# One function table in a page loop, an output norm moved up, and the last steps of a recurrence in other slots

## The chip, the cores and the metric

The kernel runs on one core of a Trainium2 chip. The metric is the device time of one launch in microseconds (us), as the median of several runs. Before the change it was 1774.12 us (three runs, 1769.87 to 1775.15).

## The reference, cut to what matters

The kernel computes one inference step of a hybrid decoder layer for a prompt of 512 tokens and for 8 decoding sequences that share the weights. Two parts of it are worked on at the same time in the loop that is changed.

The first is the latent attention of the 8 decoding sequences over their cached pages, 32 pages of 128 rows each. The keys are made from the cached rows, normalised per head, and scored:

```python
def page_step(carry, phys):
    c_blk = ckv_pool[phys]
    kp_blk = kpe_pool[phys]
    s = mla_scores(q_nope, q_pe, mla_keys(c_blk, p), kp_blk)   # mla_keys: rms_norm(c @ W) per head
    return update(carry, s, c_blk), None                       # running softmax
```

The second is the chunked gated-delta recurrence of the prompt (4 heads). Its triangular inverse is built level by level, then per chunk, with `state` carried on:

```python
v_new = u_i - w_i @ s
o = q_i @ s + a_i @ v_new
s = s * exp(gl) + k_i.T @ v_new
y = rms_norm(o, g) * silu(z)
```

Both norms are a reciprocal root, which the kernel computes on ScalarE as exp(-0.5 * ln(mean + eps)). The softmax needs exp as well.

## The kernel before, in words

The pages' loop has four iterations. One iteration takes two sequences, that is 64 pages, and one chunk of the recurrence. The 64 pages are the slots 0 to 63 of the iteration; slots 0 to 31 belong to the first sequence (r = 0), slots 32 to 63 to the second (r = 1). The order of the work on every engine is written out by hand: in each slot an engine does its part of one page and then whatever small steps the tables of slot numbers (`S_K` ... `S_OT`, `S_LVL`, `SLOT_*`) place there. Engines wait for each other by semaphores.

The page itself is a pipeline. In slot n TensorE (PE) first transposes page n + 1 (`turn_page`, L1324 to L1326; L1324 only in odd slots), then multiplies page n by the key weights (`page_products`, two groups of six matmuls, L1343; in odd slots also two small ones, L1341). ScalarE (ACT) copies the transposed page n + 1 out of the bank (`take_high`, L1511), VectorE (DVE) makes the low part of it (`take`, L1673; for even pages also a copy, L1672), and the products of page n + 1 in the next slot wait for that. ACT then squares the products of page n (L1523, L1526), and DVE sums the squares (L1683). What an engine has to do besides for its slot comes after this, and so stands in front of the next page's L1511 or L1673.

The steps that come besides are these. `values` on PE in slots 9 to 17 and 41 to 49 (L1357), `latent` in slots 19 and 51 (L1366). `soften` on ACT: Ln in slots 0 and 32 (L1478), Exp in slots 1 and 33 (L1481), the softmax's four Exps in slots 7 and 39 (L1486); on DVE the four instructions of the maximum in slots 2 and 34 (L1583 to L1588). The recurrence (`gdn`) has its PE matmuls in the slots of the tables: keys and values transposed in slots 3 and 5 (L1376, L1382), levels of the inverse at `S_LVL` (first number L1409 on PE and a copy L1493 on ACT; second number L1415 and L1418 on PE, then DVE steps L1636 in that slot and L1640 in the one after), then W, U, Q, O, S and the transposed output OT (L1453). The DVE steps at the end of a chunk are: the output's second term added (L1643 and L1647), squared (L1650), summed (L1653), the state scaled (L1656) and added to (L1659), the output normalised (L1662) and, after OT, multiplied by the gate (L1665). ACT does Ln (L1502) and Exp (L1505) of the output norm.

ScalarE evaluates a function from a table set that has to be loaded. The kernel asks for the set `exp_and_others` ahead of the loop, by `exp_only` (L265); every Ln in the loop then has an ACT_TABLE_LOAD ahead of it, and so has the Exp behind it. `log_exp` (L261) asks for the set `natural_log_exp_and_others`, which holds both; other blocks of the kernel use it.

After the loop the softmax of the last sequence is done once more by the same lines (L1478, L1481, L1583 and so on), with nothing else to do; then the next block starts.

Of the kernel before, what the change touches and what calls it, by code (L numbers as in the profile page):

```python
# [131 lines left out]
def build_in(nc, io, ctx):  # L132
# [130 lines left out]
    def exp_only(act):  # L263

        nc.scalar.preload_act_table_set("exp_and_others")  # L265
# [968 lines left out]


    S_K, S_V, S_A, S_QK, S_L0 = 3, 5, 6, 7, 10
    S_LVL = [(13, 16), (19, 22), (25, 28), (31, 35), (41, 44), (47, 50)]
    S_W, S_U, S_Q, S_O, S_S, S_OT = 52, 54, 55, 57, 58, 63
    assert len(S_LVL) == LEVELS - 1 and S_OT < 2 * PAGES

    p_w = sem("weights_split")
    with nc.Block() as block:
        @block.sync
        def _(sp):

            sp.wait_ge(p_w, 1)
            sp.dma_start(qpair[0:RO, :, 0, :], qps).then_inc(sem("pair_in"), 16)
            sp.dma_start(qpair[RO:P, :, 1, :], qps).then_inc(sem("pair_in"), 16)
            sp.wait_ge(sem("pair_in"), 32)

        @block.vector
        def _(dve):
            st = Steps(dve, sem("prelude_dve"))
            nc.vector.memset(qpair, 0.0).then_inc(p_w, 1)
            for k in range(2):
                raw = w3[:, k, :, :]
                for n, (dst, lo, hd) in enumerate(((wka4, H, 0), (wkb4, 0, 2))):
                    hi_v = dst[:, 0, k, lo:lo + 2 * HD].rearrange("p (h w) -> p h w", h=2)
                    lo_v = dst[:, 1, k, lo:lo + 2 * HD].rearrange("p (h w) -> p h w", h=2)
                    st(nc.vector.tensor_copy(hi_v, raw[:, hd:hd + 2, 0:HD]))  # L1260
                    st(nc.vector.tensor_tensor(lo_v, raw[:, hd:hd + 2, 0:HD], hi_v.bitcast(F32), ALU.subtract))
                st(nc.vector.tensor_copy(wvv[:, k, :].rearrange("p (h w) -> p h w", h=H), raw[:, :, HD:2 * HD]))
            st(nc.vector.tensor_copy(qsplit5[:, 0, :, :, :].rearrange("p b k h -> p (b k h)"), keep[:, 0:64]))
            st(nc.vector.tensor_tensor(qsplit5[:, 1, :, :, :].rearrange("p b k h -> p (b k h)"), keep[:, 0:64],
                                       qsplit5[:, 0, :, :, :].rearrange("p b k h -> p (b k h)").bitcast(F32), ALU.subtract))
            for v in (bank[0], bank[1], bank[4], bank[5], state):
                nc.vector.memset(v[:], 0.0)
            dve.sem_inc(loop_ready, 1)
            dve.sem_inc(p_e, PAGE_CREDIT)
            dve.sem_inc(p_r, PAGE_CREDIT)  # L1270
            dve.sem_inc(g_st, 1)
            dve.sem_inc(g_y, 1)
            dve.sem_inc(b_lat, 1)

        @block.gpsimd
        def _(pool):
            for v in (cpage[1][:, 0:PAGES // 2, :], ssq[1], nope[1], lat, score):
                nc.gpsimd.memset(v[:], 0.0)

        @block.scalar  # L1280
        def _(act):
            exp_only(act)
            other = cpage[1][:, PAGES // 2:PAGES, :].rearrange("p n c -> p (n c)")
            nc.scalar.activation(other, bc(ones[:, 0:1], P, PAGES // 2 * KL), ACT.Copy, scale=0.0)
            act.sem_inc(p_qa, 1)
            act.sem_inc(p_qb, 1)

        @block.tensor
        def _(pe):
            pe.sem_inc(p_kb, PAGE_CREDIT)  # L1290
            pe.sem_inc(b_pv, 1)
            pe.sem_inc(g_qs, 1)

    with nc.Block() as block:
# [177 lines left out]
        @block.scalar  # L1472
        def _(act):
            def soften(slot, m, q):

                if slot == SLOT_SOFT:
                    act.wait_ge(p_r, m * PAGES + PAGE_CREDIT)
                    nc.scalar.activation(ssq[q][:], ssq[q][:], ACT.Ln, scale=1.0 / HD, bias=eps[:]).then_inc(sem("soft_ln"), 1)  # L1478
                if slot == SLOT_SOFT + 1:
                    act.wait_ge(sem("soft_ln"), m + 1)  # L1480
                    nc.scalar.activation(ssq[q][:], ssq[q][:], ACT.Exp, scale=-0.5).then_inc(b_rs, 1)  # L1481
                if slot == SLOT_EXP:
                    act.wait_ge(b_nb, m + 1)
                    act.wait_ge(b_pv, m + 1)
                    for h in range(H):
                        nc.scalar.activation(prob[:, :, h], score[:, :, h], ACT.Exp, bias=pmax[:, 8 + h:9 + h], scale=MLA_SCALE,  # L1486
                                             accum_out=rsum[:, bass.ds(m, 1), h]).then_inc(b_exp, 1)

            def gdn(slot, c):
                for n, (sm, sd) in enumerate(S_LVL):  # L1490
                    if slot == sm:
                        act.wait_ge(g_m, c * (LEVELS - 1) + (n + 1))
                        nc.scalar.activation(mlev.rearrange("p h w -> p (h w)"), G1[:], ACT.Copy).then_inc(g_mr, 1)  # L1493
                if slot == S_W:
                    act.wait_ge(g_w, c + 1)
                    nc.scalar.activation(wneg.rearrange("p h w -> p (h w)"), G0[:], ACT.Copy, scale=-1.0).then_inc(g_we, 1)
                if slot == S_U:
                    act.wait_ge(g_vn, c + 1)
                    nc.scalar.activation(vnew, G1[:], ACT.Copy).then_inc(g_vne, 1)
                if slot == S_S + 2:  # L1500
                    act.wait_ge(g_ss, c + 1)
                    nc.scalar.activation(osm[:, 0:4], osm[:, 0:4], ACT.Ln, scale=1.0 / HD, bias=eps[0:CH, :]).then_inc(sem("gdn_ln"), 1)  # L1502
                if slot == S_S + 3:
                    act.wait_ge(sem("gdn_ln"), c + 1)
                    nc.scalar.activation(osm[:, 4:8], osm[:, 0:4], ACT.Exp, scale=-0.5).then_inc(g_rs, 1)  # L1505

            def take_high(i, r, n):
                g = i * (2 * PAGES) + (r * PAGES + n)
                act.wait_ge(p_t, g + 1)
                act.wait_ge(p_kb, page_free(g))  # L1510
                nc.scalar.activation(turned[n % 2][:, 0:KL], bank[n % 2][:, 0:KL], ACT.Copy).then_inc(p_hi, 1)  # L1511

            take_high(0, 0, 0)
            with act.Fori(0, NB // 2) as i:
                for r in range(2):
                    b = 2 * i + r
                    for n in range(PAGES):
                        g = i * (2 * PAGES) + (r * PAGES + n)
                        take_high(i, r, n + 1)
                        act.wait_ge(p_ka, g + 1)  # L1520
                        act.wait_ge(p_r, page_free(g))
                        key_at, score_at = (H, 0) if r == 0 else (0, 2 * HD)
                        nc.scalar.activation(square[n % 2][:, 0:2 * HD], bank[2][:, key_at:key_at + 2 * HD], ACT.Square)  # L1523
                        nc.scalar.activation(nope[r][:, n, :], bank[2][:, score_at:score_at + H], ACT.Copy).then_inc(p_qa, 1)
                        act.wait_ge(p_kb, page_done(g))
                        nc.scalar.activation(square[n % 2][:, 2 * HD:4 * HD], bank[3][:, 0:2 * HD], ACT.Square).then_inc(p_qb, 1)  # L1526
                        soften(n, b, 1 - r)
                        gdn(r * PAGES + n, i)
            soften(SLOT_SOFT, NB, 1)
            soften(SLOT_SOFT + 1, NB, 1)  # L1530
            soften(SLOT_EXP, NB, 1)
# [44 lines left out]
        def _(dve):  # L1576
# [32 lines left out]
            def gdn(slot, c):  # L1609
# [34 lines left out]
                if slot == S_O:  # L1644
                    dve.wait_ge(g_av, c + 1)
                    dve.wait_ge(g_o1, c + 1)
                    nc.vector.tensor_tensor(o1, G1[:], o1, ALU.add).then_inc(chain, 1)  # L1647
                if slot == S_S:
                    dve.wait_ge(chain, c * 3 + 1)
                    nc.vector.tensor_tensor(osq, o1, o1, ALU.mult).then_inc(chain, 1)  # L1650
                if slot == S_S + 1:
                    dve.wait_ge(chain, c * 3 + 2)
                    nc.vector.tensor_reduce(osm[:, 0:4], heads(osq), AX, ALU.add).then_inc(g_ss, 1)  # L1653
                if slot == S_S + 2:
                    dve.wait_ge(g_kv, c + 1)
                    nc.vector.tensor_tensor(heads(state), heads(state), col(elast[:, bass.ds(c * H, H)], P, H, HD), ALU.mult).then_inc(chain, 1)  # L1656
                if slot == S_S + 3:
                    dve.wait_ge(chain, c * 3 + 3)
                    nc.vector.tensor_tensor(state, G0[:], state, ALU.add).then_inc(g_st, 1)  # L1659
                if slot == S_OT - 1:  # L1660
# [862 lines left out]
```

## Time and profile before

| | us |
|---|---|
| median of three runs | 1774.12 (1769.87 to 1775.15) |
| profiled execution, its own time | 1768.66 |
| span in the profile | 1766.9 |
| PE busy | 1571.0 (89%) |
| DVE busy | 812.6 (46%) |
| ACT busy | 656.7 (37%) |

The profiled execution is 5.5 us shorter than the median of the runs. The busy shares are means over the whole kernel; the changed loop runs from about 395 to 1056 us after the span's start, and in it PE has hardly any gap. PEld is TensorE's weight load, which comes ahead of each matmul; where a row of it has an idle time in brackets, PE had nothing to go on with.

### The profile page before, as it was taken

The numbers are of one execution on the slowest core, as the hardware profiler recorded it, in microseconds if no ns is written. First come the engines' busy times: TensorE is split into PE (matmuls) and PEld (weight loads), VectorE is DVE, ScalarE is ACT, GpSimd is POOL, SyncE is SP. The second block draws the span as 40 slices with busy tenths as digits, with TensorE's granted clock in tenths as the row PEclk, the third lists the DMA queues.
The fourth block names the chain that finished last, engine by engine and source line by source line (L and its number), as shares of the span: only waits on it lengthen the run. The fifth ranks groups of instructions, "written<-read, shape, count | busy, mean of one in ns | idle before, by whom it ended". The sixth has DMA issues, their size and how long they took to land. (4 is left out here: it accounts for less than half of the span.)

```text
span 1766.9 us, 31133 instructions
## 1 busy us (share of the span) xinstructions
PE 1571.0 (89%) x10945; PEld 1300.4 (74%) x10945; DVE 812.6 (46%) x1552; ACT 656.7 (37%) x1660; POOL 65.0 (4%) x77
## 2 busy tenths in 40 slices
PE   2999667619998999899989997999888999998999
PEld 2599434318988898888989883534443999998998
DVE  2311577765555554655565551332566222224321
ACT  3022234445545555545454560000123333334121
POOL 0000000030000000000000000000000000000000
PEclk8999886869999999999999997899889999999999
DMA  7022000022313131313222207124203233331331
GB/s 235 0 75 69 15 0 1 23 63 54 91 42 89 39 93 45 89 38 87 53 70 57 65 1 257 59 63 187 107 1 97 72 95 95 95 86 50 89 102 55
DMA packets 190622, 128.29 MB, mean 73 GB/s; under 512 B 49240, under 2 KB 175953, under 8 KB 190468
## 3 DMA queue, kind: packets, MB, share of 16 engines
q1 hardware_dynamic: 190476, 126.52, 24.8%
q8 instruction: 70, 1.15, 0.3%
q14 instruction: 76, 0.62, 0.1%
HBM read 120.20 MB, written 6.37 MB: 72 GB/s over the span
## 5 line engine op out<-in xcount | busy, mean ns | idle before, releaser
L1343 PE MATMUL bank<-wka,turned 128*128 128x260 f32 x1536 | 252.4, 300 | 15.9 <-DVE turned L1673 13.8
L1683 DVE TENSOR_REDUCE arena<-arena 128x4 f32<-128x512 f32 x256 | 175.6, 686 | 183.9 <-ACT arena L1526 183.3
L1343 PE MATMUL bank<-wkb,turned 128*128 128x256 f32 x1536 | 237.6, 291 | 0.0
L1343 PEld LDWEIGHTS bank<-wka,turned 128*128 128x128 f32 x1536 | 203.2, 192 | 27.1 <-DVE turned L1673 24.5
L1343 PEld LDWEIGHTS bank<-wkb,turned 128*128 128x128 f32 x1536 | 202.7, 192 | 0.0
L2276 PE MATMUL bank<-h_high,ffn_high 128*128 128x260 f32 x704 | 142.5, 284 | 3.0 <-DVE h_low L2334 3.0
L2276 PE MATMUL bank<-h_low,ffn_high 128*128 128x260 f32 x704 | 142.7, 284 | 0.0
L2276 PE MATMUL bank<-h_high,ffn_low 128*128 128x260 f32 x704 | 142.1, 284 | 0.0
L1511 ACT ACTIVATE turned<-bank 128x256 fp32r<-128x256 f32 x257 | 98.3, 382 | 109.2 <-PE bank L1326 109.2
L1673 DVE TENSOR_TENSOR turned<-bank,turned 128x256 fp32r<-128x256 f32 x257 | 107.1, 417 | 56.1 <-ACT turned L1511 56.1
L1526 ACT ACTIVATE arena<-bank 128x256 f32<-128x256 f32 x256 | 98.7, 386 | 89.4 <-PE bank L1343 89.4
L1523 ACT ACTIVATE arena<-bank 128x256 f32<-128x256 f32 x256 | 98.3, 384 | 80.1 <-PE bank L1343 78.5
L1750 PE MATMUL bank<-arena,yT 128*128 128x512 f32 (+1 forms) x240 | 121.7, 644 | 4.3 <-DMA arena<-in_w_mix_out 3.9
L2276 PEld LDWEIGHTS bank<-h_high,ffn_high 128*128 128x128 f32 x704 | 109.4, 190 | 3.1 <-issue 3.1
L2276 PEld LDWEIGHTS bank<-h_low,ffn_high 128*128 128x128 f32 x704 | 109.1, 190 | 0.0
L2276 PEld LDWEIGHTS bank<-h_high,ffn_low 128*128 128x128 f32 x704 | 109.0, 189 | 0.0
L2318 DVE TENSOR_TENSOR ffn_low<-arena,ffn_high 128x1024 fp32r<-128x1024 f32 x43 | 52.6, 1225 | 84.7 <-ACT ffn_high L2285 84.7
L1750 PEld LDWEIGHTS bank<-arena,yT 128*128 128x128 f32 (+1 forms) x240 | 40.4, 183 | 58.3 <-issue 47.5
L1325 PE MATMUL bank<-con,arena 128*128 128x128 f32 x257 | 72.8, 283 | 9.5 <-issue 9.5
L2411 PE MATMUL bank<-act_high,down_high 128*128 128x260 f32 x352 | 73.2, 290 | 5.8 <-DVE act_low L2485 5.8
L2411 PE MATMUL bank<-act_low,down_high 128*128 128x260 f32 x352 | 72.4, 288 | 0.0
L2285 ACT ACTIVATE ffn_high<-arena 128x1024 fp32r<-128x1024 f32 x43 | 45.5, 1060 | 72.2 <-DMA arena<-in_ffn_w_gate 59.0
(413 smaller groups left out, 2611.3 us busy)
## 6 DMA issues: line engine op xcount, KB each, us to landing
arena<-in_cache_mla_ckv SPq DMA_DIRECT2D x256, 128.0 KB, 2.0
arena<-in_ffn_w_gate SPq DMA_DIRECT2D x22, 512.0 KB, 4.0
arena<-in_ffn_w_up SPq DMA_DIRECT2D x22, 512.0 KB, 5.2
arena<-in_ffn_w_down SPq DMA_DIRECT2D x16, 704.0 KB, 5.0
arena<-in_w_in SPq DMA_DIRECT2D x16, 512.0 KB, 3.8
arena<-in_cache_mla_kpe SPq DMA_DIRECT2D x256, 32.0 KB, 1.8
arena<-in_x_prompt SPq DMA_DIRECT2D x8, 512.0 KB, 6.3
arena<-in_w_mix_out SPq DMA_DIRECT2D x2, 2048.0 KB, 11.3
```

The lines of the kernel that those rows point to most:

```text
L1325: nc.tensor.transpose(b[:, 0:P], cpage[r][:, n, 0:P], ident)
L1343: last = nc.tensor.matmul(dst, t[:, (2 * part + k) * P:(2 * part + k + 1) * P], w4[:, wpart, k, cl], start=(m == 0), stop=(m == len(SPLIT) ...
L1511: nc.scalar.activation(turned[n % 2][:, 0:KL], bank[n % 2][:, 0:KL], ACT.Copy).then_inc(p_hi, 1)
L1523: nc.scalar.activation(square[n % 2][:, 0:2 * HD], bank[2][:, key_at:key_at + 2 * HD], ACT.Square)
L1526: nc.scalar.activation(square[n % 2][:, 2 * HD:4 * HD], bank[3][:, 0:2 * HD], ACT.Square).then_inc(p_qb, 1)
L1673: nc.vector.tensor_tensor(t[:, KL:2 * KL], bank[n % 2][:, 0:KL], t[:, 0:KL].bitcast(F32), ALU.subtract).then_inc(p_e, 1)
L1683: nc.vector.tensor_reduce(ssq[r][:, n, :], square[n % 2].rearrange("p (h w) -> p h w", h=H), AX, ALU.add).then_inc(p_r, 1)
L1750: last = nc.tensor.matmul(bank[n % 2][0:rows, :], self.lhs[:, k, t * P:t * P + rows], self.w[:, k, a * 512:(a + 1) * 512], start=(k == 0), ...
L2276: last = nc.tensor.matmul(bank[4 * c + 2 * u + j][:, 0:HALF_T], fw[wp][2 * c + u][:, k, :], hp[rp][:, k, j * HALF_T:(j + 1) * HALF_T], sta ...
L2285: nc.scalar.activation(fr_high[s][:], fring[s].rearrange("p k n -> p (k n)"), ACT.Copy).then_inc(f_wh, 1)
L2318: nc.vector.tensor_tensor(fr_low[s][:], fring[s].rearrange("p k n -> p (k n)"), fr_high[s][:].bitcast(F32), ALU.subtract).then_inc(f_w, 1)
L2411: last = nc.tensor.matmul(bank[2 * c + j][:, 0:HALF_T], dw[wp][n][:, k, :], ap[rp][:, kk_, j * HALF_T:(j + 1) * HALF_T], start=(kk_ == 0 a ...
```

## The change

Three things are changed in the pages' loop.

1. The set asked for ahead of the loop is `natural_log_exp_and_others` in place of `exp_and_others`.
2. The output norm of the recurrence is counted from `S_O` (the output) and no more from `S_S` (the state): square, sum, Ln and Exp stand in the four slots right behind the output, and the state's two DVE steps come in slots `S_S` + 1 and + 2.
3. The last two levels lie in slots (39, 43) and (46, 49) in place of (41, 44) and (47, 50), and all that follows is one or two slots earlier, OT in slot 62 in place of 63.

```diff
-    S_LVL = [(13, 16), (19, 22), (25, 28), (31, 35), (41, 44), (47, 50)]
-    S_W, S_U, S_Q, S_O, S_S, S_OT = 52, 54, 55, 57, 58, 63
+    S_LVL = [(13, 16), (19, 22), (25, 28), (31, 35), (39, 43), (46, 49)]
+    S_W, S_U, S_Q, S_O, S_S, S_OT = 51, 53, 54, 55, 57, 62
...
         @block.scalar
         def _(act):
-            exp_only(act)
+            log_exp(act)
...
-                if slot == S_S + 2:
+                if slot == S_O + 3:
                     act.wait_ge(g_ss, c + 1)
                     nc.scalar.activation(osm[:, 0:4], osm[:, 0:4], ACT.Ln, ...
-                if slot == S_S + 3:
+                if slot == S_O + 4:
                     act.wait_ge(sem("gdn_ln"), c + 1)
                     nc.scalar.activation(osm[:, 4:8], osm[:, 0:4], ACT.Exp, scale=-0.5).then_inc(g_rs, 1)
...
-                if slot == S_S:
+                if slot == S_O + 1:
                     dve.wait_ge(chain, c * 3 + 1)
                     nc.vector.tensor_tensor(osq, o1, o1, ALU.mult).then_inc(chain, 1)
-                if slot == S_S + 1:
+                if slot == S_O + 2:
                     dve.wait_ge(chain, c * 3 + 2)
                     nc.vector.tensor_reduce(osm[:, 0:4], heads(osq), AX, ALU.add).then_inc(g_ss, 1)
-                if slot == S_S + 2:
+                if slot == S_S + 1:
                     dve.wait_ge(g_kv, c + 1)
                     nc.vector.tensor_tensor(heads(state), heads(state), ...
-                if slot == S_S + 3:
+                if slot == S_S + 2:
                     dve.wait_ge(chain, c * 3 + 3)
                     nc.vector.tensor_tensor(state, G0[:], state, ALU.add).then_inc(g_st, 1)
```

On ACT, at the start of a sequence, the loads in front of Ln and Exp are gone (the difference in ACT's order; L1511 is the next page's copy):

```order
 L1526 ACTIVATE arena<-bank 128x256
 L1477 ISA
-L1478 ACT_TABLE_LOAD
 L1478 ACTIVATE arena<-arena,eps 128x128
 L1511 ACTIVATE turned_2495<-bank 128x256
```

In the program as written eight such rows go: two loads for each of the two sequences of an iteration, two for the output norm, and two after the loop.

Also on ACT, behind the last of the softmax's four Exps of the second sequence (L1486, slot 39), there stood the work of two pages before the copy of the next level (L1493):

```order
L1486 ACTIVATE arena,keep<-arena 128x33
L1511 ACTIVATE turned_2496<-bank 128x256
L1523 ACTIVATE arena<-bank 128x256
L1524 ACTIVATE arena<-bank 128x4
L1525 REGISTER_ALU
L1526 ACTIVATE arena<-bank 128x256
```

In the changed kernel the copy follows the Exps at once, ahead of the next page's L1511:

```order
L1486 ACTIVATE arena,keep<-arena 128x33
L1492 REGISTER_ALU
L1493 ACTIVATE arena<-bank 128x512
L1511 ACTIVATE turned_2496<-bank 128x256
L1523 ACTIVATE arena<-bank 128x256
```

On PE, the end of an iteration was this (L1453 is OT, the four transposes of the normalised output; L1457 is the loop's branch):

```order
L1330 REGISTER_ALU
L1343 MATMUL bank<-wka,turned_2496 128x260 x6
L1341 MATMUL bank<-arena 128x8
L1343 MATMUL bank<-wkb,turned_2496 128x256 x6
L1453 MATMUL bank<-con,arena 128x128 x4
L1457 REGISTER_ALU
L1457 COMPARE_AND_BRANCH
```

In the changed kernel it is this:

```order
L1326 MATMUL bank<-con,arena 128x128
L1330 REGISTER_ALU
L1343 MATMUL bank<-wka,turned_2495 128x260 x6
L1343 MATMUL bank<-wkb,turned_2495 128x256 x6
L1453 MATMUL bank<-con,arena 128x128 x4
L1320 REGISTER_ALU
L1324 MATMUL bank<-con,arena 128x128
```

L1453 has moved from behind the products of slot 63 to behind those of slot 62, a slot without L1341.

## Rows read from the trace of the kernel before

**Rows 1.** Windows of the loop: busy us (instructions) by engine, granted clock, DMA, GB/s.
```profile
560.00:640.00 80.00, 77.20 (x647) 71.37 (x648) 43.84 (x95) 41.50 (x137) 5.99 (x8) 0.96 0.23 62
...
sum 662.00, PE 636.95 PEld 584.14 DVE 372.26 ACT 359.40 POOL 47.03; mean PE 79.62 PEld 73.02 DVE 46.53 ACT 44.92 POOL 5.88
```
**Rows 2.** Waits of PEld, 396 to 1057 us: us in total, times, longest.
```profile
PEld bank L1343 <- DVE turned L1673: 24.5, 41, 1.2
```
**Rows 3.** Groups by line, ACT: count | busy us, mean ns | idle before.
```profile
L1478 ACT ACT_TABLE_LOAD x9 | 11.5, 1283 | 0.2
...
L1502 ACT ACT_TABLE_LOAD x4 | 5.1, 1283 | 0.1
```
**Rows 4.** Timeline, slots 32 to 35, first iteration: start us, us, instruction [idle before].
```profile
478.93 1.28 ACT L1478 ACT_TABLE_LOAD   x1
...
481.13 0.41 DVE L1673 TENSOR_TENSOR turned<-bank,turned 128x256 fp32r<-128x256 f32 x1
...
481.60 0.78 PEld L1343 LDWEIGHTS bank<-wka,turned 128*128 128x128 f32 x6 [1.15 <-DVE turned L1673]
...
483.91 0.77 PEld L1343 LDWEIGHTS bank<-wka,turned 128*128 128x128 f32 x6 [0.51 <-DVE turned L1673]
```
**Rows 5.** Timeline of PEld, the other waits of the first iteration.
```profile
404.39 0.78 PEld L1343 LDWEIGHTS bank<-wka,turned 128*128 128x128 f32 x6 [0.99 <-DVE turned L1673]
...
491.60 0.77 PEld L1343 LDWEIGHTS bank<-wka,turned 128*128 128x128 f32 x6 [0.35 <-DVE turned L1673]
497.83 0.78 PEld L1343 LDWEIGHTS bank<-wka,turned 128*128 128x128 f32 x6 [0.80 <-DVE turned L1673]
...
551.26 0.78 PEld L1343 LDWEIGHTS bank<-wka,turned 128*128 128x128 f32 x6 [0.38 <-DVE turned L1673]
553.80 0.78 PEld L1343 LDWEIGHTS bank<-wka,turned 128*128 128x128 f32 x6 [0.64 <-DVE turned L1673]
556.00 0.78 PEld L1343 LDWEIGHTS bank<-wka,turned 128*128 128x128 f32 x6 [0.41 <-DVE turned L1673]
```
**Rows 6.** Timeline of DVE, a level's step in slot 36.
```profile
490.33 0.68 DVE L1640 TENSOR_TENSOR arena<-arena,bank 128x512 f32<-128x512 f32 x1
...
490.93 0.28 DVE L1672 COPY arena<-bank 128x128 f32<-128x128 f32 x1
```
**Rows 7.** Timeline: four transposes in slot 3, the maximum's DVE steps in slot 34.
```profile
406.04 0.46 PEld L1376 LDWEIGHTS bank<-con,arena 128*128 128x128 f32 x4
...
484.65 0.28 DVE L1583 TENSOR_TENSOR arena<-arena 128x128 f32<-128x128 f32 x1
...
485.67 0.28 DVE L1672 COPY arena<-bank 128x128 f32<-128x128 f32 x1
```
**Rows 8.** Timeline: behind the Exps of slot 7; a level's copy on ACT.
```profile
417.51 0.42 DVE L1673 TENSOR_TENSOR turned<-bank,turned 128x256 fp32r<-128x256 f32 x1 [0.32 <-ACT turned L1511]
...
418.05 0.77 PEld L1343 LDWEIGHTS bank<-wka,turned 128*128 128x128 f32 x6
...
476.87 0.60 ACT L1493 ACTIVATE arena<-bank 128x512 f32<-128x512 f32 x1 [0.51 <-PE bank L1409]
```
**Rows 9.** Timeline, slots 59 and 60: a DVE step, and PE one page on.
```profile
550.20 0.68 DVE L1653 TENSOR_REDUCE keep<-arena 128x4 f32<-128x512 f32 x1
...
550.52 0.14 PEld L1324 LDWEIGHTS bank<-con,arena 128*128 128x128 f32 x1
```
**Rows 10.** Timeline behind the loop.
```profile
1056.79 0.69 DVE L1683 TENSOR_REDUCE arena<-arena 128x4 f32<-128x512 f32 x1 [0.44 <-ACT arena L1526]
...
1058.07 0.40 ACT L1478 ACTIVATE arena<-arena,eps 128x128 f32<-128x128 f32 x1
...
1060.13 0.29 DVE L1583 TENSOR_TENSOR arena<-arena 128x128 f32<-128x128 f32 x1 [2.05 <-ACT arena L1481]
```
**Rows 11.** Timeline of PEld at the first return to the loop's start.
```profile
561.80 0.18 PEld L1325 LDWEIGHTS bank<-con,arena 128*128 128x128 f32 x1 [3.67 <-issue]
...
562.24 1.37 PEld L1343 LDWEIGHTS bank<-wka,turned 128*128 128x128 f32 x6
```

## The prediction

> **What bounds the kernel now.** I read the sums over windows of the loop first: of 662 us PE is busy 637, DVE 372, ACT 359 [rows 1]. So the loop is PE's, and no engine beside it is full; a change on ACT and DVE can gain only where PE waits for them. The view of waits, for PE's weight loads, names that place: 41 waits of L1343 for L1673, 24.5 us together [rows 2]. No other wait of PE for an engine is listed in the loop. The timeline says which slots they fall in. In each iteration they come in five kinds, and their counts add up to the 41:
>
> - behind the two table loads at slots 32 and 33: 1.15 and 0.51 us [rows 4], four times, 6.6 us;
> - behind those at slots 0 and 1: 0.99 us [rows 5], in one or two waits per iteration, five in all; some 4.6 us together;
> - at the end of the recurrence (slots 61 to 63): 0.38, 0.64 and 0.41, four times, 5.7 us [rows 5];
> - behind the four Exps of slot 39: 0.80, four times, 3.2 us [rows 5];
> - behind a DVE step of a level (slots 23, 29, 36): 0.35 at 491.60 for the last of them [rows 5], twelve, 4.4 us by what is left of the 24.5.
>
> **The rule behind the small waits.** Take the step L1640 in slot 36. It holds DVE for 0.60 us, from its start to that of the next L1672 [rows 6], and the products two pages on, at 491.60, wait 0.35 [rows 5]. So a slot in which PE has nothing but its page, followed by another such slot, hides 0.25 us of extra DVE work, and the rest is paid by PE. Any extra PE work in those two slots (the 0.46 of four transposes [rows 7], or the matmuls of a level) hides that much more; and a wait that PE has already paid one page earlier hides as well.
>
> **Part 1: the table.** By the ACT rows 9 loads stand at L1478 and 4 at L1502, 1.283 us each [rows 3], and as many again at the Exps behind them (L1481, L1505): 26 loads, 33.4 us of ACT. The order shows all of them gone and none added but the one ahead of the loop, which takes the place of another. ACT's 33 us don't count, PE's waits do. With the loads away, the Ln left at slots 0 and 32 takes 0.40 us [rows 10] and the Exp at 1 and 33 no more, and ACT has idle time in each page (359 busy of 662). So kinds one and two go: 11.2 us. What is late next is DVE's maximum in slots 2 and 34: 1.02 us from the first step to the next L1672 [rows 7], 0.77 more than the 0.25 that is hidden. In slot 35 PE has the two groups of a level, which cover it. In slot 3 it has only the 0.46 us of transposes [rows 7], so 0.31 us is left to wait, four times: 1.2 us. In the trace before it doesn't show, since PE has just waited the 0.99 us. Kinds one and two save 10.0 us.
>
> After the loop the chain is bare. The last sum ends at 1057.48, the Ln starts at 1058.07 and DVE's L1583 at 1060.13 [rows 10]. Without the first load the Ln starts at 1057.50. From the Ln's end to L1583 lie 1.66 us, of which 1.28 are the second load. So L1583 comes at 1057.50 + 0.40 + 0.38 = 1058.3, 1.85 us earlier. The transposes of the output, which were done behind the last page and beside this chain, now stand ahead of the last page's products: 0.46 us back, by the same four transposes in slot 3 [rows 7]. The tail gives 1.4 us.
>
> The Trainium skill ("ScalarE: Activation LUTs", What ACT_TABLE_LOAD costs) puts 1283 ns on the load and some 1380 ns of drain beside it, about 2.66 us for each switch. This case's trace agrees on the load and has no room for the drain: 2.66 us and an Exp don't fit into the 1.66 us of [rows 10]. By the page the tail would give 2.8 us more, and the sum below would be 18.1 in place of 15.3; I go by the rows.
>
> **Part 2: the end of the recurrence.** DVE's steps stand at 54 to 59, 61 and 62 in place of 55 and 57 to 63. In slots 54, 55 and 57 PE has matmuls of its own, so the square in 56 and the sum in 57 are covered. The state's scaling in 58 has two bare slots behind it and costs the 0.35 of slot 36; the addition in 59 profits from that wait and leaves under 0.1. The normalisation in 61 has OT in slot 62 to cover it. So 1.43 becomes 0.35 us, four times: 4.3 us saved. Bounds: nothing saved, if these three steps wait their 1.43 without the loads too, and all 5.7.
>
> The price is a new wait. OT (L1453) needs the normalised output of the slot before. Before, slot 63 was an odd one with L1341 in it, and PE came late enough. Now the same distance has to be kept over slot 62, an even one. The same pair, an odd slot with a DVE step and then an even slot on PE, stands in the trace at 59 and 60: the DVE step ends at 550.88, while PE has finished the next page's products at 550.52 [rows 9]. With the 0.06 us that L1343 takes behind the end of L1673 [rows 4] OT waits 0.42 us, four times: 1.7 us. Bounds: 0 (if DVE gets ahead of its page) and four times the 1.15 of [rows 4], the longest wait of PE here.
>
> **Part 3: the levels.** The waits at slots 23, 29 and 36 stay (4.4 us). In slot 39 ACT has four Exps and now also a level's copy; PE has a level's four matmuls there, which it hadn't. The nearest rows are slot 7, with the Exps and four PE matmuls of that size but no copy: DVE ends at 417.93, PE goes on at 418.05 without a wait, 0.12 us to spare [rows 8]. The copy takes 0.60 us [rows 8], so PE waits up to 0.48 in place of 0.80: four times, 1.3 us saved. Bounds: all 3.2 saved, if the matmuls cover the copy too; 0.8 lost, if the copy is also held up by the 0.51 us for its matmuls as in [rows 8], 0.99 a time. The other moved levels keep three slots or more between PE, ACT, GpSimd and PE, and lie beside `values`, as before. U to O loses a slot (54 to 57 becomes 53 to 55); ACT's copy between them needs 0.60 us, and a page lasts 2.6 on average (662 us [rows 1] for 256 pages), so nothing waits.
>
> **Sum.** PE's waits before 24.5; after 4.4 (levels) + 1.2 (slot 2) + 1.4 (slot 58) + 1.7 (OT) + 1.9 (slot 39) = 10.6. That is 13.9 saved, and 1.4 in the tail: 15.3 us. The work of PE is the same. The profiled execution took 1768.66, so it would take 1753.4. The runs' median lies 5.5 above the profiled one; from 1774.12 the same saving gives 1758.8, which is my prediction.
>
> **Rivals.**
> - *No new waits.* OT, slots 2, 39 and 58 are all covered by slack that I don't see, since waits shift each other. Then only the levels' 4.4 remain: 24.5 - 4.4 + 1.4 = 21.5 saved, 1752.6. For it: each wait that PE pays gives the other engines a page of rest. Against it: slot 36 pays its 0.35 with nothing ahead of it.
> - *The waits come back.* With the loads gone DVE is the next to be late at the same places, so half of the loads' 11.2 us stays in slots 0 to 3 and 32 to 35 (5.6, of which 1.2 are in the sum), and the end of the recurrence pays its 1.43 still: 15.3 - 4.4 - 4.3 = 6.6 saved, 1767.5. For it: DVE has steps in every slot from 2 to 7. Against: in slots 0, 1, 32 and 33 it has none.
> - *Slower, by the clock.* At the loop's return PE idles 3.67 us and then runs on at the lower level, 1.2 GHz: six weight loads take 1.37 us [rows 11] where they take 0.78 [rows 5]; the granted clock of the window with this return is 0.96 of full speed [rows 1]. Two such sets a page make 1.2 us per page. The new wait at OT lies one page ahead of that idle time. If it lengthens the low stretch, the saving of 15.3 is gone after 13 more pages at the low level, and from 17 on (some six per return) the kernel is slower by over 0.3%; with 20 pages it takes 1783. The Trainium skill ("TensorE: Matmul & The Clock Gate", Part 1) has the low level as the default, which activity lifts; the trace agrees so far as PE goes back to the fast rows. Against it: 0.4 us is little beside 3.67, and PE is busier elsewhere.
>
> That the change doesn't do what it says I leave out: the order shows the loads gone.
>
> **How the numbers follow.** Forecast 0.68, no new waits 0.16, waits come back 0.12, slower 0.04. About 0.3%, or 5.3 us, is what a measurement of this kernel can tell from no change. The first two are faster, and of the third most; a start from the profiled execution's 1768.66 or the runs' 1775.15 moves any of them by some five, so I put 0.07 on no change: faster 0.89, same 0.07, slower 0.04. The range goes from the largest saving on the shortest execution, 1768.66 - 21.5 = 1747, to the third case, 1767.5: 1747 to 1768.
>
> **What would show it.** No ACT_TABLE_LOAD between the loop's first page and the next block. PEld's wait for L1673 at some 9 us in place of 24.5, with none of 1 us; a new PE wait for L1662 of about 1.7 us in four. The wait behind slot 39 near 0.5. The loop about 14 us shorter with PE's busy time unchanged, L1583 about 0.8 us behind the last sum. It is wrong if PE waits at L1343 for over 15 us, if waits for L1453 pass 4 us, or if the low clock behind the loop's returns grows.

## The result

The changed kernel took 1745.01 us (median of four runs, 1744.74 to 1754.42), the kernel before, on the same chip, 1772.35 (four runs, 1769.87 to 1775.15): ratio 0.9858, 95% interval 0.9821 to 0.9895. Run once more on another chip (changed_again, below) it had a ratio of 0.9893 (0.9879 to 0.9907). It is faster, by more than the 15.3 us that were forecast: the medians differ by 27.3. The prediction was 1758.8, and 1745.0 lies 2 us under the lower end of its range; by the ratio, from the 1774.12 that the forecast started from, it is 1748.9, inside.

### The profile after

The profiled execution took 1744.74 us, 23.9 less than the one before. The first view is the waits of TensorE's weight loads and, below the "...", of its matmuls, with the totals, the number of times and the longest, in us. The first row answers to [rows 2].

```profile
PEld bank L1325 <- issue: 18.6, 31, 2.2
PEld bank L1343 <- DVE turned L1673: 8.7, 24, 0.4
...
PE bank L1325 <- issue: 5.8, 3, 2.0
...
PE bank L1453 <- DVE arena L1662: 0.9, 4, 0.2
```

PE's waits for L1673 went from 24.5 us in 41 to 8.7 us in 24, and none is longer than 0.4. The timeline of PEld shows where they are in the first iteration: behind slot 2, behind a level's step (slot 23, twelve such in the loop), behind slots 39 and 58; then the new wait of OT, and the loop's first return. They answer to [rows 5, 11].

```profile
406.04 0.30 PEld L1343 LDWEIGHTS bank<-wka,turned 128*128 128x128 f32 x2 [0.34 <-DVE turned L1673]
...
459.26 0.30 PEld L1343 LDWEIGHTS bank<-wka,turned 128*128 128x128 f32 x2 [0.37 <-DVE turned L1673]
...
495.87 0.30 PEld L1343 LDWEIGHTS bank<-wka,turned 128*128 128x128 f32 x2 [0.37 <-DVE turned L1673]
...
546.63 0.30 PEld L1343 LDWEIGHTS bank<-wka,turned 128*128 128x128 f32 x2 [0.36 <-DVE turned L1673]
...
552.19 0.20 PEld L1453 LDWEIGHTS bank<-con,arena 128*128 128x128 f32 x2 [0.41 <-issue]
...
556.78 0.14 PEld L1325 LDWEIGHTS bank<-con,arena 128*128 128x128 f32 x1 [2.15 <-issue]
```

The last row is the surprise: at the return PE sat idle 2.15 us, where it had sat 3.67 [rows 11]. The two later returns fell too, from 3.10 and 3.41 to 2.02 and 2.22; together 10.2 us became 6.4.

Behind the loop the chain of [rows 10] is now:

```profile
1037.53 0.69 DVE L1683 TENSOR_REDUCE arena<-arena 128x4 f32<-128x512 f32 x1 [1.04 <-ACT arena L1526]
1038.25 0.40 ACT L1478 ACTIVATE arena<-arena,eps 128x128 f32<-128x128 f32 x1 [0.75 <-DVE arena L1683]
1038.68 0.31 ACT L1481 ACTIVATE arena<-arena 128x128 f32<-128x128 f32 x1
1039.03 0.29 DVE L1583 TENSOR_TENSOR arena<-arena 128x128 f32<-128x128 f32 x1 [0.81 <-ACT arena L1481]
```

No table load stands between the Ln (L1478) and the Exp (L1481), and L1583 comes 0.81 us behind the sum's end; before it was 2.65.

Where the 23.9 us are, between three marks of the two traces: the loop's first product of a page (L1343), the first transfer issue of the next block (L1802), and that block's L1900. Windows of the next block's start before (two rows) and after (two rows), with the span in us, busy time by engine, granted clock, DMA share and GB/s:

```profile
1071.70:1100.00 28.30, 24.02 (x60) 12.78 (x61) 3.27 (x13) 2.79 (x5) 0.00 (x0) 0.76 1.00 343
1100.00:1130.00 30.00, 30.00 (x112) 19.82 (x111) 7.49 (x12) 2.18 (x7) 0.00 (x0) 0.77 0.38 142
```

```profile
1050.90:1079.20 28.30, 23.84 (x64) 12.79 (x65) 3.26 (x13) 2.93 (x5) 0.00 (x0) 0.82 0.99 341
1079.20:1109.20 30.00, 30.00 (x115) 18.46 (x113) 8.44 (x14) 2.05 (x6) 0.00 (x0) 0.83 0.39 143
```

| stretch | before | after | difference |
|---|---|---|---|
| loop and its tail, L1343 to L1802 | 395.55 to 1071.7 = 676.1 | 395.66 to 1050.9 = 655.2 | -20.9 |
| next block, L1802 to L1900 | 53.9 | 50.7 | -3.2 |
| all else | | | +0.2 |

The loop's 20.9 is made up of: waits for L1673 -15.8; wait of OT +1.6; tail -1.4 (L1583 stands 1.84 sooner behind the last sum, and OT's 0.46, once beside that chain, now lies ahead of it); idle at the returns -3.8; and -1.2 behind the returns, where the stretch from PE's going on to slot 3, less its waits for L1673, fell from 28.2 to 27.0 us over the three, 1.1 of it at the first. That leaves 0.3, or 0.6, since from L1583 to L1802 the tail took 11.9 us in place of 11.6. The next block's 3.2 us go with a higher granted clock (0.82 in place of 0.76) for the same work; the change doesn't touch that block.

### The profile page after: what moved, and what is told of

It is laid out like the page before. It is cut to its first block and busy times, and to the rows that moved or that the text cites. A ratio compares the mean times of both kernels' runs of the same rounds, so it can differ in the third digit from the quotient of the medians.

```text
span 1743.0 us, 31107 instructions
## 1 busy us (share of the span) xinstructions
PE 1561.1 (90%) x10945; PEld 1295.2 (74%) x10945; DVE 809.7 (46%) x1552; ACT 625.9 (36%) x1634; POOL 64.9 (4%) x77
## 5 line engine op out<-in xcount | busy, mean ns | idle before, releaser
L1343 PE MATMUL bank<-wka,turned 128*128 128x260 f32 x1536 | 251.3, 300 | 4.1 <-DVE turned L1673 1.1
L1343 PE MATMUL bank<-wkb,turned 128*128 128x256 f32 x1536 | 237.3, 291 | 0.0
L1343 PEld LDWEIGHTS bank<-wka,turned 128*128 128x128 f32 x1536 | 202.9, 192 | 10.9 <-DVE turned L1673 8.7
L1343 PEld LDWEIGHTS bank<-wkb,turned 128*128 128x128 f32 x1536 | 202.3, 191 | 0.0
L1511 ACT ACTIVATE turned<-bank 128x256 fp32r<-128x256 f32 x257 | 98.1, 382 | 109.8 <-PE bank L1326 109.7
L1526 ACT ACTIVATE arena<-bank 128x256 f32<-128x256 f32 x256 | 98.2, 383 | 97.5 <-PE bank L1343 97.5
L1673 DVE TENSOR_TENSOR turned<-bank,turned 128x256 fp32r<-128x256 f32 x257 | 107.0, 417 | 45.7 <-ACT turned L1511 45.7
L1325 PE MATMUL bank<-con,arena 128*128 128x128 f32 x257 | 72.6, 282 | 5.8 <-issue 5.8
L2411 PE MATMUL bank<-act_high,down_low 128*128 128x260 f32 x352 | 72.1, 287 | 0.0
```

Source lines behind the costliest of these rows:

```text
L1325: nc.tensor.transpose(b[:, 0:P], cpage[r][:, n, 0:P], ident)
L1343: last = nc.tensor.matmul(dst, t[:, (2 * part + k) * P:(2 * part + k + 1) * P], w4[:, wpart, k, cl], start=(m == 0), stop=(m == len(SPLIT) ...
L1673: nc.vector.tensor_tensor(t[:, KL:2 * KL], bank[n % 2][:, 0:KL], t[:, 0:KL].bitcast(F32), ALU.subtract).then_inc(p_e, 1)
L2411: last = nc.tensor.matmul(bank[2 * c + j][:, 0:HALF_T], dw[wp][n][:, k, :], ap[rp][:, kk_, j * HALF_T:(j + 1) * HALF_T], start=(kk_ == 0 a ...
```

## The experiments

Two theories on the surplus. **Theory R**: PE's idle time at the return counts from the last semaphore that PE's queue has to wait for. Before, OT stood behind the last page's products and waited for L1662, and that was the last; now OT stands one page earlier. **Its rival**: the returns got shorter because ACT's program lost its table loads, or because of which instructions stand last. "The loop" below is always L1343 to L1802 as in the table.

### The two halves: table_only and slots_only

```diff
# table_only: the kernel before, with
-            exp_only(act)
+            log_exp(act)
# slots_only: the changed kernel, with
-            log_exp(act)
+            exp_only(act)
```

> The kernel before with the one function table alone; every slot stays. Theory: PE's idle time at the loop's three returns counts from the last semaphore that PE's queue has to wait for, some 4.2 us, and the output's transposes at the end of slot 63 are such a wait; so the returns stay at 3.1 to 3.7 us (10.2 in all, against 6.4 with the whole change). Rival: ACT's shorter program makes the returns short; then they are 2.0 to 2.2 here too. In both PEld's waits for L1673 fall from 24.5 to about 12 (levels 4.4, Exps of slot 39 3.2, slot 2 1.2, end of the recurrence 3), and the tail gives 1.9: 14 to 15 us less than before, 18 by the rival.

> The changed kernel with only its first part undone: the set asked for ahead of the loop is exp_and_others again, so every Ln of the loop and the Exp behind it has its table load; the slots and the norm stay as changed. Theory W (PE's idle time at the loop's return is set by the last wait that PE's queue passes, and so by where the transposed output stands): the three returns stay at 2.0 to 2.2 us, though the loads are back. The loads cost what they cost before: 10.0 us at slots 0 to 3 and 32 to 35, 4 to 6 us at the output norm, 1.4 us behind the loop, so the loop takes some 655.2 + 16 = 671 us and the whole 14 to 18 us more than the changed kernel. Rival (the returns got shorter because ACT's program has fewer instructions or fewer table loads): returns of 2.9 to 3.5 us, the loop at 675 us.

| | time, us | ratio to before | loop | waits for L1673 | idle at the three returns |
|---|---|---|---|---|---|
| table_only | 1754.37 | 0.9905 (0.9885 to 0.9926) | 661.5 | 12.0 in 28 | 3.43, 2.85, 3.47 |
| slots_only | 1764.63 | 0.9969 (0.9954 to 0.9983) | 671.8 | 23.5 in 39 | 2.14, 2.16, 1.89 |

The first return in the timeline of PEld, with the table alone, and then with the slots alone:

```profile
563.79 0.18 PEld L1325 LDWEIGHTS bank<-con,arena 128*128 128x128 f32 x1 [3.43 <-issue]
```

```profile
561.01 0.14 PEld L1325 LDWEIGHTS bank<-con,arena 128*128 128x128 f32 x1 [2.14 <-issue]
```

Both as theory R had it: the table takes away waits and leaves the returns (one, 2.85, a little under the 3.1 expected), the slots shorten the returns though every table load is back. The loop's savings are 14.6 and 4.3 us, 18.9 of the 20.9. slots_only took 13.5 us more than the changed kernel on the same chip (changed_again), where 14 to 18 were expected. With the loads, the new slots save only 1.0 us of waits for L1673. In the first iteration the end of the recurrence waits 1.43 us before, 1.46 with the slots alone (1.05 and 0.41), 0.76 with the table alone (0.38 twice) and 0.36 with both: the table brings the larger part of what was forecast for the slots there.

### Where the last wait stands: ot63_norm62, ot63_norm61, late_wait

```diff
# ot63_norm62: the changed kernel, OT back in slot 63 (and the norm in 62)
-    S_W, S_U, S_Q, S_O, S_S, S_OT = 51, 53, 54, 55, 57, 62
+    S_W, S_U, S_Q, S_O, S_S, S_OT = 51, 53, 54, 55, 57, 63
# ot63_norm61: the same, and the norm a slot earlier
-                if slot == S_OT - 1:
+                if slot == S_OT - 2:
# late_wait: the changed kernel; in slot 63 PE waits for page 63's last square
+                        if r * PAGES + n == 2 * PAGES - 1:
+                            pe.wait_ge(p_qb, i * (2 * PAGES) + 2 * PAGES + 1)
```

> The whole change, but the output normalised in slot 62 and its transposes in slot 63, as before. Theory (the return counts from the last wait): the returns go back to 3.1 to 3.7 us, the 1.6 us that PE waits for L1662 go, L1673 stays at 8.7; the kernel is 1.5 to 3 us slower than with the whole change. Rival (what group stands last decides): the same here. Rival (ACT's program): returns stay 2.0 to 2.2, and the kernel is some 2 us faster than with the whole change.

> As ot63_norm62, but the output is normalised in slot 61, two slots ahead of its transposes in slot 63, whose semaphore has then passed long before. Theory (the return counts from the last wait): the last wait is that of the products of slot 63, and 0.46 us more of work stands behind it, so the returns are 1.6 us each, and no wait for L1662: 3 to 4 us faster than with the whole change. Rival (what group stands last decides): returns 3.1 to 3.7 as before.

> The whole change with one wait more: at the end of each iteration, behind the products of slot 63, PE waits for the last square of that page (some 0.7 us after PE's last product). Theory (the return counts from the last wait): returns at 0.7 + 4.2 = 4.9 us each in place of 2.1, so the loop is 8 us longer, and perhaps more at the low clock. Rival (what group stands last decides, or ACT's program): returns unchanged at 2.0 to 2.2.

| | time, us | ratio to before | loop | idle at the three returns |
|---|---|---|---|---|
| ot63_norm62 | 1751.02 | 0.9889 (0.9868 to 0.9911) | 658.5 | 3.35, 3.65, 3.50 |
| ot63_norm61 | 1747.39 | 0.9863 (0.9839 to 0.9887) | 655.1 | 2.37, 1.97, 2.05 |
| late_wait | 1759.2 | 0.9936 (0.9918 to 0.9955) | 665.2 | 4.67, 4.32, 4.33 |

The end of the iteration in late_wait (its lines behind L1467 stand two further down, so L1528 is the square of L1526), all engines:

```profile
555.19 0.38 ACT L1528 ACTIVATE arena<-bank 128x256 f32<-128x256 f32 x1 [0.47 <-PE bank L1343]
555.60 0.69 DVE L1685 TENSOR_REDUCE arena<-arena 128x4 f32<-128x512 f32 x1 [1.03 <-ACT arena L1528]
559.62 0.18 PEld L1325 LDWEIGHTS bank<-con,arena 128*128 128x128 f32 x1 [4.67 <-issue]
```

A wait that asks for no work of PE's adds 2.1 to 2.5 us to each return, and the loop is 10 us longer, where 8 were expected; the granted clock of the 4.2 us behind each return is 0.50, where the changed kernel has 0.59 to 0.62. At the first return PE's next instruction comes 4.05 us behind the square's end. The same distance, from the end of what the last wait waits for, is 4.38 us before (L1662), 4.37 after (L1673 of page 63, the row below), 4.28 with the table alone and 3.88 in ot63_norm62. Over all three returns of these and the other looped kernels it lies between 3.7 and 4.6, so it isn't a fixed time.

```profile
551.99 0.42 DVE L1673 TENSOR_TENSOR turned<-bank,turned 128x256 fp32r<-128x256 f32 x1
```

In ot63_norm62 the returns are long again, and the loop is 3 us longer than in the changed kernel (1.5 to 3 expected). With OT last and its input early (ot63_norm61) the idle is 2.0 to 2.4: what stands last in the program doesn't count, what is waited for last does. I had expected 1.6 there and a loop 3 to 4 us shorter. The idle is that of the changed kernel because the last wait (L1673 of page 63, ending at 556.67) has the same 2.4 us of PE's work behind it, to 559.09. The loop is the same too, since PE now waits 0.38 four times behind the norm in slot 61, which has no extra work of PE's behind it, as the rule of the prediction would have told.

### Is there a floor: long_tail_con

```diff
+                        if r * PAGES + n == 2 * PAGES - 1:
+                            pe.wait_ge(g_st, i + 2)
+                            for k in range(6):
+                                nc.tensor.matmul(G0[:], ident, con[:, 0:512], start=True, stop=True)
```

> The changed kernel with six more matmuls of 512 columns on PE at the end of slot 63, into a bank that is not read again, from data that never change; they wait for nothing that is late. By the four transposes of 128 columns (0.46 us) one takes some 0.43 us, six 2.6 us. Theory W1 (the next iteration's first instruction comes a fixed 4.2 to 4.4 us behind the last wait that PE's queue passes, whatever PE does meanwhile): the added work lies inside that time, the idle at the returns falls from 2.1 to about 0, and the loop grows by 0.5 us at each of three returns and 2.6 at its end, some 4 us in all. Theory W2 (there is also a floor of about 2 us behind the last instruction of the iteration): idle stays at 2.0 to 2.2 us and the loop grows by 4 x 2.6 = 10.4 us.

Measured: 1749.43 us, ratio 0.9875 (0.9861 to 0.9889). The timeline of PE at the first return:

```profile
559.55 0.94 PE L1343 MATMUL bank<-wkb,turned 128*128 128x256 f32 x6
560.34 5.31 PE L1471 MATMUL bank<-con 128*128 128x512 f32 x12
565.49 0.27 PE L1325 MATMUL bank<-con,arena 128*128 128x128 f32 x1
```

The six matmuls stand there as twelve, 5.2 us and not 2.6, and the next iteration follows them with no idle time at all. So there is no floor, and W2 falls; the two us seen so often are what remains of some four when PE has about two us of work behind its last wait. One iteration, from the wait behind slot 2 to the next such (411.70 to 573.69), takes 162.0 us against 160.9 in changed_again (407.24 to 568.11): 5.2 us of work more for 1.1 us. The 4.1 us that cost nothing are the idle time, 2.25 there, and a rest of some 1.8 us, which I put down to the low clock. For the 4.2 us behind the return the window of the changed kernel shows a granted clock of 0.61, a mixture of the levels 1.2 and 2.4 GHz (first row), and that of this run 1.00 (second):

```profile
556.80:561.00 4.20, 4.20 (x21) 3.99 (x22) 1.27 (x3) 1.86 (x6) 0.00 (x0) 0.61 0.32 86
```

```profile
565.50:569.70 4.20, 4.20 (x37) 4.20 (x36) 1.64 (x4) 2.60 (x10) 0.00 (x0) 1.00 0.28 82
```

### Taking the returns away: pe_two, straight_three

```diff
# pe_two: PE alone, two iterations to a round
-            with pe.Fori(0, NB // 2) as i:
+            with pe.Fori(0, NB // 4) as two:
+                for i in (2 * two, 2 * two + 1):
# straight_three: PE, ACT and DVE written out
-            with pe.Fori(0, NB // 2) as i:
+            for i in range(NB // 2):
...
```

> The changed kernel with PE's loop alone written as two rounds of two iterations, so that PE returns once (between the second and the third iteration) and no more three times; the work and its order are the same. In the changed kernel a return costs PE 2.1 us idle and, by the run with the longer tail, some 1.9 us at the low clock behind it. Theory A (the returns cost what they do because of the jump, on each engine): the idle at the ends of the first and third iteration goes, the one in the middle stays at 2.0 to 2.4; but ACT returns there still, and its copy of page 1 (L1511) came 2.86 us behind ACT's last wait. So PE waits some 2.2 us for page 1 (L1343 for L1673) at the first and third end in place of the idle time, and gains 0 to 2 us a time, 0 to 4 in all. Theory B (only PE pays for the return): no such wait, the loop 8 us shorter. Theory C (the idle time isn't of the jump but of something else at the iteration's end): idle of 2.0 to 2.4 us at all three ends, nothing gained.

> The changed kernel with the four iterations written out one behind the other on PE, ACT and DVE, so that none of the three returns; GpSimd and the queue of transfers keep their loops. The work and its order are the same. Theory A (the jump is what costs): no idle time of PE over 0.5 us at the three ends, no low clock behind them, 3 x (2.1 + 1.9) = 12 us gained: loop 643 in place of 655.3. Rival (straight code four times as long costs as much by its loading, or what the loop hid at its ends comes out as waits for L1673): 4 us or less gained.

pe_two took 1744.08 us, ratio 0.9843 (0.9827 to 0.986), loop 654.1. At the first end of an iteration, the last transpose of page 1 and ACT's timeline, then PE's wait for ACT (on ACT and DVE the lines are one further down; L1512 is the copy L1511):

```profile
560.36 0.27 PE L1326 MATMUL bank<-con,arena 128*128 128x128 f32 x1
560.45 0.38 ACT L1527 ACTIVATE arena<-bank 128x256 f32<-128x256 f32 x1 [0.49 <-PE bank L1343]
563.50 0.38 ACT L1512 ACTIVATE turned<-bank 128x256 fp32r<-128x256 f32 x1 [2.67 <-issue]
```

```profile
564.60 0.19 PEld L1343 LDWEIGHTS bank<-wka,turned 128*128 128x128 f32 x1 [2.45 <-DVE turned L1674]
...
721.68 0.14 PEld L1325 LDWEIGHTS bank<-con,arena 128*128 128x128 f32 x1 [2.17 <-issue]
```

PE runs on past the first end, and then waits 2.45 us (2.64 at the third) for page 1, because ACT, which still returns, stood still for 2.67 with nothing to wait for: the transpose that it copies had ended at 560.63. In the middle, where PE returns too, its idle of 2.17 is there. That is theory A, and the gain is 1.2 us.

straight_three took 1736.1, ratio 0.9803 (0.9788 to 0.9817), loop 644.6: 10.7 us less than the changed kernel, where 12 were expected. No idle of PE over 0.4 us for L1325 is left, the granted clock around the three ends is 1.00, and the waits for L1673 are the old 24 and one of 1.1 us at the loop's entry:

```profile
PEld bank L1325 <- issue: 12.2, 28, 0.4
PEld bank L1343 <- DVE turned L1673: 9.9, 25, 1.1
```

The Trainium skill ("Runtime: NRT & Kernel Launch", Instruction fetch mechanics) says that a taken branch to code outside the window the sequencer holds forces a fetch before the engine can go on, and that kernels therefore prefer to be unrolled. The traces agree so far as PE and ACT stall at the branch and do not where it is gone; the fetch itself no run here shows.

### A better version: norm60_level_early, straight_norm60

```diff
-    S_LVL = [(13, 16), (19, 22), (25, 28), (31, 35), (39, 43), (46, 49)]
-    S_W, S_U, S_Q, S_O, S_S, S_OT = 51, 53, 54, 55, 57, 62
+    S_LVL = [(13, 16), (19, 22), (25, 28), (31, 35), (40, 43), (46, 49)]
+    S_W, S_U, S_Q, S_O, S_S, S_OT = 51, 53, 54, 55, 57, 61
...
-                    if slot == sd + 1 and whole:
+                    if slot == sd and whole:
```

> A version built from what the runs showed. Against the changed kernel: the output norm's last step in slot 60 and the transposed output in 61, so that a slot with work of PE's lies behind neither; the second DVE step of each level (L1640) in the level's own slot, where PE has eight matmuls (1.1 to 1.3 us), and no more in the bare slot behind it; the fifth pair of the levels (40, 43) in place of (39, 43), so that the level's copy on ACT is not behind the four Exps. By the rule of the prediction: the levels' twelve waits (4.4 us) go, the four behind slot 39 (1.5 us) go, the wait for L1662 falls from 1.6 us to 0.4 or less, those of slots 2 and 58 stay (2.8 us). The returns stay at 2.0 to 2.2. So L1673's waits fall from 8.7 us in 24 to some 3 in 8, the loop from 655.2 to 648, and the whole takes 6 to 8 us less than the changed kernel. Rival (two DVE steps in one slot, 1.3 us, are too much for it, or the Exps of slot 39 wait as they did before, 0.80 four times): 3 to 6 us of waits come back, and the time is within 3 us of the changed kernel.

> The version norm60_level_early with PE, ACT and DVE written out in the same way. There the three returns showed 2.53, 2.70 and 2.48 us of idle time. Theory A: 3 x (2.55 + 1.9) = 13 us gained on that version's loop of 647.9, so some 635, and the whole some 18 to 22 us below the changed kernel. Rival: 4 us or less gained, the loop at 644 or more.

norm60_level_early: 1740.97 us, ratio 0.9835 (0.9817 to 0.9854), loop 647.9, against 1751.15 and 655.5 of the changed kernel on the same chip. Its waits:

```profile
PEld bank L1343 <- DVE turned L1673: 2.8, 8, 0.4
...
PEld bank L1324 <- DVE turned L1673: 1.7, 4, 0.4
```

The eight waits left are those of slots 2 and 58, as the rule has it, and OT waits no more. The second row was not foreseen: two DVE steps in slot 43 hold back a transpose (L1324), 0.43 us four times. Nor was it foreseen that the returns would rise to 2.53, 2.70 and 2.48. They fit theory R all the same. With OT gone from slot 62, PE's last wait is for the square of page 62 (L1526), whose bank the second group of slot 63 needs:

```profile
551.37 0.38 ACT L1526 ACTIVATE arena<-bank 128x256 f32<-128x256 f32 x1 [0.26 <-PE bank L1343]
...
555.62 0.14 PEld L1325 LDWEIGHTS bank<-con,arena 128*128 128x128 f32 x1 [2.53 <-issue]
```

It ends at 551.75, and PE goes on 3.87 us later; but only 1.55 us of PE's work stand behind it (to 553.30), where the changed kernel has 2.43.

straight_norm60, the same with PE, ACT and DVE written out: 1727.66 us (1725.29 to 1731.77), ratio 0.9767 (0.9749 to 0.9785), loop 637.3, 10.5 us less than with the loop, where 13 were expected. It is the fastest kernel of these runs, 8.4 us below straight_three on the same chip.

### The same kernel again: changed_again

> The changed kernel once more, beside the others on the same chip. If the 3.1 us by which the stretch behind the loop (from the next block's first transfer issue to L1900) was shorter than before is the clock of that one execution and not the change, this stretch lies anywhere between 50 and 54 us here and the granted clock in it anywhere between 0.76 and 0.83, while the loop stays at 655 (within 2) and the three returns at 2.0 to 2.2 us. If it belongs to the change, it is 50.7 us again, and over 53 us in every kernel with the loads or the slots of before.

1751.15 us (four runs, 1746.04 to 1752.22); loop 655.5, returns 2.25, 1.88 and 2.38, waits for L1673 8.8 in 24: the loop repeats to 0.3 us. The next block took 50.6 us, nearly the 50.7 again, which by itself would speak for the change. But by the same expectation it should then be over 53 wherever the loads or the slots of before are back, and it is 49.4 with the table alone, 49.1 with the slots alone, 51.0 and 51.1 in ot63_norm62 and ot63_norm61, 52.5 in long_tail_con. It goes up and down without the change, and with the granted clock: over the thirteen traces this block takes 49.1 to 49.5 us where the part from 28.3 us behind L1802 on is granted 0.84, 50.6 to 51.2 us at 0.77 or 0.78, and 52.2 to 53.9 at 0.71 to 0.73. What sets the clock there stays open.

## Why the prediction was right in the loop and short in the sum

- **The table, right.** The waits of the first two kinds went; slot 2 kept four of 0.34 (forecast 0.31). With the table alone the loop fell by 14.6 us.
- **What is left of the waits, right in size and place.** Forecast: 8.9 us in 24 waits of four named kinds. Measured: 8.7 in 24, of the same kinds, 0.34 to 0.38 each. Slot 39 was put at 0.48 and is 0.37.
- **The new wait of OT, right.** 0.41 us four times, 1.6 in all, against 1.7.
- **The tail, right.** L1583 stands 0.8 us behind the sum, 1.84 us sooner; less OT's 0.46 that is 1.4 us. The drain of the Trainium skill ("ScalarE: Activation LUTs", What ACT_TABLE_LOAD costs), by which the tail would have given 2.8 us more, doesn't show in what the tail gained either.
- **The slots' part, right only together with the table.** Part 2 gave the slots 4.3 us at the end of the recurrence. The table alone brings 2.7 of them there (1.43 to 0.76, four times), the slots the rest; in the sum this doesn't show.
- **Wrong: "The work of PE is the same".** The work is, but the sum left the loop's return out: it has no term for a change of the idle time there, and gives no reason. It was looked at in one place only, the rival of the low clock, and with the wrong sign: the new wait one page ahead of the return was taken for a danger, when moving the last wait a page ahead is what shortens the return. It gave 3.8 us of idle; another 1.2 us were saved behind the returns, 5.0 in all. That these 1.2 us come of the shorter idle isn't shown (see the last section). The low clock behind the returns didn't grow: from the return to slot 3 the granted clock was 0.72, 0.84 and 0.83 before, 0.81 three times after. The place could be read from the trace before. DVE's timeline has the step that OT waited for, and PE went on 4.4 us behind its end [rows 11], with little but the rest of the page and OT to do in between:

```profile
556.74 0.68 DVE L1662 TENSOR_TENSOR arena<-arena,keep 128x512 f32<-128x512 f32 x1
```

- **Not of the change.** 3.2 us in the next block, which go with its clock. And the 5.5 us that I added to go from the profiled execution to the median weren't there in the changed kernel, whose profiled time is its median. Over all traces the loop's first product stands either at 395.5 to 396.7 us (eight) or at 399.6 to 401.2 (five), whichever kernel it is, so such a step belongs to the execution. 1758.8 less 5.3 (20.6 found in place of 15.3), 3.2 and 5.5 is 1744.8; 1745.0 was measured. That it closes so well is luck, as executions of one kernel differ by more. Of the 13.8 us that I was off, about 5 are the returns that I missed, and the rest is what two executions differ by; in changed_again the time was 1751.15, inside the range.

## What to carry to other kernels

A short wait in a software pipeline could be forecast here to about a tenth of a us from the slot's extra work on the slow engine, less what the fast one has to do besides in that slot and the next. A loop's return has a price, and on PE it runs here from the last semaphore that the engine waits for in the body: let that wait come early, put work that waits for nothing behind it, or write the loop out, on the engines that hand each other the pages and not on PE alone. Set the sum against marks inside the trace as well as against the median, since blocks that a change doesn't touch move by some us from one execution to the next.

## What the runs showed of the hardware

- At the first return of a loop of some 2700 PE instructions the next instruction of PE came 3.9 to 4.5 us behind the end of what its last wait waited for, in seven kernels (before, after, table_only, ot63_norm62, ot63_norm61, late_wait, norm60_level_early); over all their returns it is 3.7 to 4.6. 5.2 us of matmuls queued behind that wait hid it wholly (long_tail_con). ACT stood still 2.67 us at its return (pe_two). Written out, both run on.
- Behind some of these idle times PE goes on at the low clock, behind others not, and the length of the idle doesn't tell which: the 4.2 us behind an idle of 2.15 (changed kernel) had a granted clock of 0.61, behind 2.17 (pe_two, middle) 1.00, behind 2.53 and 2.70 (norm60_level_early) 1.00 and 0.71. In the first case the clock was 1.00 up to the end of the idle time and fell behind it. What decides it stays open.
